# Fused two-block kernel: the last quarter of the first query weights loaded into weight buffer 0, query blocks 12 to 15 at rows 7 to 10

## What is computed

```python
def block(hb):                       # hb: 128 tokens
    q = (hb @ w_pq).reshape(TOK_BLOCK, PEER_HEADS, 2, PEER_DHALF)
    s = jnp.einsum('thpd,hpnd->thpn', q, sub_keys)
    s1, i1 = lax.top_k(s[:, :, 0], PEER_TOPK)
    s2, i2 = lax.top_k(s[:, :, 1], PEER_TOPK)
    ...
    idx = jnp.take_along_axis(cand_i, pos, axis=-1)
    gate = jax.nn.softmax(top_s, axis=-1)
    u = expert_u[idx]
    act = jax.nn.gelu(jnp.einsum('thkd,td->thk', u, hb), approximate=False)
    return jnp.einsum('thk,thkd->td', gate * act, expert_v[idx])
```

## Time and profile before

| | us |
|---|---|
| three timed runs | 2435.77, 2431.96, 2430.18 |
| median | 2431.96 |
| the profiled execution, its own time | 2429.78 |
| its span, first to last instruction | 2428.0 |
| around the span | 1.8 |

### The profile page before, as it was taken

The page is one execution under the profiler, slowest core; times in us unless marked ns, Lnnn a source line. Parts: engine busy times, 40 slices in busy tenths (PEclk is TensorE's granted clock), DMA queues, the critical chain, the costliest instruction groups (busy, mean ns, idle before and its releaser), DMA issues.

```text
span 2428.0 us, 34184 instructions
## 1 busy us (share of the span) xinstructions
PE 2081.3 (86%) x12956; PEld 1589.9 (65%) x12956; DVE 1543.4 (64%) x3428; ACT 1211.8 (50%) x2391; POOL 802.9 (33%) x684
## 2 busy tenths in 40 slices
PE   6989998897797886666669999776998999989998
PEld 4445576786555655555567788645887757858863
DVE  5565665688865677788566686566666544955422
ACT  1123331466657667666676567767776740111110
POOL 2000000365643333455544895333332310800000
PEclk9999888998898998666679999987999999999999
DMA  4322245788899999999999999999999975353431
GB/s 169 121 96 69 73 146 206 285 325 306 352 354 395 415 418 415 420 421 419 417 418 415 414 362 417 415 418 414 409 413 412 412 297 193 113 189 107 172 139 69
DMA packets 162133, 729.71 MB, mean 301 GB/s; under 512 B 10161, under 2 KB 13361, under 8 KB 95921
## 3 DMA queue, kind: packets, MB, share of 16 engines
q0 software_dynamic: 73728, 536.90, 54.7%
q1 hardware_dynamic: 88240, 190.62, 21.5%
HBM read 725.38 MB, written 2.10 MB: 300 GB/s over the span
## 4 chain that ended last, share of the span: by engine, by line
PE 45%; DMA 25%; DVE 15%; ACT 9%; issue 4%; POOL 2%; SPq 0%; DVEq 0%; ACTq 0%; POOLq 0%
DMA AR<-in_uv,C 19%; PE PA L923 12%; PE PD L1510 7%; PE PA L1442 4%; PE PD L923 4%; ACT AR L2026 3%; PE PA L1455 3%; DVE AR L2944 2%; DMA WR<-in_w_up 2%; DMA WR<-in_w_down 2%; DVE AR L2888 2%; PE PD L1087 2%; PE PA L1584 2%; PE PD L1584 2%; POOL AR L3179 1%
## 5 line engine op out<-in xcount | busy, mean ns | idle before, releaser
L2888 DVE CUSTOM_DVE_ANT_0 AR<-AR,HN 128x1024 f32<-128x1024 f32 x467 | 587.9, 1264 | 344.1 <-issue 180.8
L3179 POOL DMA_INDIRECT AR<-in_uv,C x467 | 558.7, 1196 | 711.7 <-PE PD L1510 669.3
L1510 PE MATMUL PD<-C,AR 128*128 128x128 f32 x3736 | 594.0, 313 | 221.1 <-ACT AR L2026 219.9
L1510 PEld LDWEIGHTS PD<-C,AR 128*128 128x128 f32 x3736 | 504.7, 162 | 351.9 <-ACT AR L2026 299.4
L2026 ACT ACTIVATE AR<-AR,SC 128x1024 f32<-128x1024 f32 x467 | 536.6, 1149 | 15.2
L2022 ACT ACTIVATE SC<-SC 128x1 f32<-128x1 f32 x512 | 103.7, 203 | 368.8 <-DVE SC L2888 367.7
L3179 POOL DMA_INDIRECT WR<-in_uv,C x45 | 52.4, 1164 | 464.1 <-DVE C L2621 394.7
L923 PE MATMUL PA<-HT,WR 128*128 128x256 f32 (+1 forms) x608 | 185.2, 465 | 0.9 <-ACT AR L2045 0.9
L1442 PE MATMUL PA<-HT,WR 128*128 128x256 f32 x704 | 168.7, 386 | 12.1 <-DMA WR<-in_w_up 12.1
L923 PE MATMUL PA<-AR,WR 128*128 128x256 f32 (+1 forms) x896 | 170.4, 353 | 0.7 <-ACT AR L1803 0.7
L923 PEld LDWEIGHTS PA<-AR,WR 128*128 128x128 f32 x896 | 152.6, 193 | 17.7 <-ACT AR L1803 1.1
(11 more groups left out here) (495 smaller groups left out, 3088.5 us busy)
## 6 DMA issues: line engine op xcount, KB each, us to landing
WR<-in_w_up SPq DMA_DIRECT2D x22, 2048.0 KB, 18.0
WR<-in_w_in SPq DMA_DIRECT2D x18, 2048.0 KB, 8.5
WR<-in_w_ada SPq DMA_DIRECT2D x12, 2048.0 KB, 8.3
WR<-in_w_down SPq DMA_DIRECT2D x9, 2048.0 KB, 9.4
WR<-in_w_pq SPq DMA_DIRECT2D x8, 2048.0 KB, 16.4
WR<-in_w_o SPq DMA_DIRECT2D x4, 2048.0 KB, 18.4
WR<-in_w_out SPq DMA_DIRECT2D x4, 2048.0 KB, 18.9
AR<-in_uv,C POOLq DMA_INDIRECT x467, 14.6
```

The lines of the kernel that those rows point to most:

```text
L1510: ins = nc.tensor.matmul(acc[i // 4][:, P * (i % 4):P * (i % 4) + P], uv_row(j, D + P * i, D + P * i + P), ident, start=(k == 0 and i % 4 ...
L2888: ttr(uv_row(j, 0, D), uv_row(j, 0, D), HN[:, t, :], 1.0, 0.0, ALU.mult, ALU.add, DOT[:, j:j + 1]).then_inc(s["dots"], 1)
L3179: nc.gpsimd.indirect_dma_start(uv_row(ring_slot(turn), 0, 2 * D), None, uv, bass.IndirectOffsetOnAxis(ap=IDX[:, t % 2, i:i + 1], axis=0),) ...
```

## The change

The fourth quarter of w_pq goes to weight buffer 0 instead of 1, behind the third. So weight buffer 1 is free once block 7 is done, and the ring has places 0, 8, 9, 10, 11 from row 0 to row 51. Blocks 12 to 15 move from rows 2, 2, 3 and 4 to rows 7, 8, 8 and 10, key score 4 from row 7 to row 13, the matrices of chunk 1 from rows 11, 13, 15 to 14, 16, 18 (and so their masks from rows 20, 22, 24 to 23, 25, 27). GpSimd's clear moves from row 5 to row 12 and waits for block 15 in place of block 11. GpSimd's wait for block 15 at row 8 becomes a wait for block 7 at row 3.

```diff
-PHASES = ((0, (8, 9, 0)), (6, (8, 9, 10, 11, 0)), (52, (9, 3, 5, 6, 0, 4, 8)), (66, (7, 3, 5, 6, 0, 4)),
+PHASES = ((0, (0, 8, 9, 10, 11)), (52, (9, 3, 5, 6, 0, 4, 8)), (66, (7, 3, 5, 6, 0, 4)),
           (96, (7, 3, 5, 6, 0, 4, 1, 2)))
...
-MATRIX_AT = {1: (11, 13, 15), 2: (33, 35, 36), 3: (39, 41, 42)}
+MATRIX_AT = {1: (14, 16, 18), 2: (33, 35, 36), 3: (39, 41, 42)}
...
-FIRST_QUERY_AT = {0: (8, 9), 1: (10, 11), 2: (12, 13), 3: (14,), 4: (15,)}
-FIRST_SCORE_AT = {4: 3, 7: 4}
+FIRST_QUERY_AT = {0: (8, 9), 1: (10, 11), 7: (12,), 8: (13, 14), 10: (15,)}
+FIRST_SCORE_AT = {4: 3, 13: 4}
+CLEAR_AT = 12
...
-        col_chunk(w_pq, 512, 512, "a", FIRST_A[("query", 7)])
-        col_chunk(w_pq, 1024, 512, "a", FIRST_A[("f", 3)])
-        col_chunk(w_pq, 1536, 512, "uv", FREED[10] - 1)
-        SLOTS += [1, 2, 0, 3, 1, 0, 1]
+        col_chunk(w_pq, 512, 512, "uv", FREED[10] - 1)
+        col_chunk(w_pq, 1024, 512, "a", FIRST_A[("query", 11)])
+        col_chunk(w_pq, 1536, 512, "a", FIRST_A[("f", 3)])
+        SLOTS += [1, 2, 0, 3, 1, 0, 0]
...
-                if row == 5:
+                if row == CLEAR_AT:
                     own_done()
-                    pool.wait_ge(s["a_full"], FIRST_A[("query", 11)] + 1)
+                    pool.wait_ge(s["a_full"], FIRST_A[("query", 15)] + 1)
                     z = WR[64:128, 0, 0:3072].rearrange("p (i n) -> p i n", i=3 * H)
                     joined(nc.gpsimd.memset(z[:, :, 0:64], 0.0), "cleared")
...
-                    if turn == 8:
-                        pool.wait_ge(s["a_full"], FIRST_A[("query", 15)] + 1)
+                    if turn == 3:
+                        pool.wait_ge(s["a_full"], FIRST_A[("query", 7)] + 1)
```

## The result

| | before | after |
|---|---|---|
| median of 8 runs each, us | 2433.93 (2428.73 to 2438.09) | 2444.51 (2440.82 to 2449.91) |
| ratio, 95% interval | | 1.0046 (1.0032 to 1.0061) |
| the profiled execution, its own time | 2429.78 | 2443.26 |
| its span | 2428.0 | 2441.5 |

The changed kernel is slower by 0.46%, some 10.6 us between the medians (the ratio is not the quotient of the two medians, which would be 1.0043). The two profiled executions differ by 13.5 us. From about L923 on, a line of the code has a number higher by one in the changed kernel (L924, L1088, L1511, L2889, L3137, L3146, L3180 for L923, L1087, L1510, L2888, L3136, L3145, L3179).

A forecast was written before the change was run, and what follows sets the result against it. TensorE's own list was taken to set the pace in rows 0 to 11, VectorE and ScalarE to make it wait after row 16. 9.0 + 2.1 + 2.3 - 4.4 = 9.0 us on 2431 gave 2440, range 2433 to 2448.

The forecast's parts named there:

- More places, gathers early: nothing gained: Dots 4 to 6: removes VectorE's gather waits, which TensorE's blocks cover; gains nothing, at most 10.8 us.
- Blocks out of rows 2 to 4: TensorE idle 1.0 us before row 5: Row 5: TensorE's list ends at 463.5, but the row is ready at 464.5, so TensorE idles 1.0 us.
- Row 8 at 475.9, block 15 done at 490.7: Rows 5 to 10 with the moved blocks: nothing won or lost, as row 11 started at 490.74 before.
- The fourth quarter: no wait: SP's w_pq load before block 12: 19.6 us available, load 16.4 in the middle; no wait taken, at most 11.1 us.
- The clear at row 12: 9.0 us: GpSimd's clear waits for block 15, gather 12 issues at 494.1, row 12 starts at 502.9, 9.0 us late.
- What is still to do and the clock: 2.1 + 2.3 us: Behind row 12: key score 4 and row 11's matrix add 2.1 us, the lower clock after idling 2.3 us.
- What is given back: 4.4 us: Rows 12 to 22: a late TensorE makes its idle time before rows 19 and 22 disappear, 4.4 us, bounds nothing to 6.6.
- Matrices and masks three rows later: no change: Chunk 1's moved masks: each costs a VectorE dot as much at its new row, so the sum stays.
- the delay given back: Rival: rows 13 to 22 make up for more of the gap, 6.6 us; 2435 to 2438 us; chance 0.21.
- the gather waits as pace: Rival: at rows 4 to 6 gather waits set the pace, so 10.8 us come off; 2429 us; chance 0.07.
- the late load: Rival: the fourth quarter's load makes block 12 wait, up to 11.1 us; 2451 us, at 22 us 2442; chance 0.08.
- held gathers: Rival: something else holds gather 3 or 4, and the gap at row 12 stays; still 2440 us; chance 0.02.

The follow-up runs named there:

- Run 4: Changed kernel with the clear at row 17 and the earlier three places in rows 0 to 5: 2440.25 us, 1.0024 of the kernel before.
- run 1: Changed kernel with GpSimd's clear at row 17 in place of row 12: 2431.6 us, 0.9992 of the kernel before.
- run 2: Kernel before with only gather 12 held until TensorE has done row 11's transposes: 2440.83 us, 1.003 of the kernel before.
- run 6: Changed kernel, clear at row 12, with chunk 1's three masks at rows 27, 29 and 31: 2441.16 us, 1.0025 of the kernel before.
- run 5: Changed kernel with the clear at row 17 and chunk 1's three masks at rows 27, 29 and 31: 2426.35 us, 0.997 of the kernel before.
- run 7: Kernel before with only chunk 1's three masks moved to rows 27, 29 and 31: 2433.53 us, 0.9996 of the kernel before.

## Why the prediction was right, and where its working was not

- **More places, gathers early: nothing gained. Right.** The waits ahead of dots 4 to 6 went, and row 5 came when TensorE's list allowed. Run 4 gives the other half: with the blocks moved and the places not, 7.4 us are lost.
- **Blocks out of rows 2 to 4: TensorE idle 1.0 us before row 5. Off by that 1.0.** Row 5 began at 463.27, with no wait in front of it; 464.5 was forecast (0.4 of the difference was there at row 0). The mis-sized term is ScalarE's 3.00 us from table load to end. The table load ran ahead of dot 5, so 1.75 us after the dot (461.13) the scaled line was there, at 462.88, before TensorE had done its list:

```profile
457.78 1.28 ACT L2023 ACT_TABLE_LOAD   x1
...
461.73 1.15 ACT L2027 ACTIVATE AR<-AR,SC 128x1024 f32<-128x1024 f32 x1
```

- **Row 8 at 475.9, block 15 done at 490.7.** 474.73 and 489.54: the durations held, and both are early by the 1.2 us of the point before.
- **The fourth quarter: no wait. Right.** Block 12 followed without idle time, and the eight loads took about what they did before: 8.0 to 29.2 us, 16.8 in the middle.

```profile
472.84 2.05 PE L924 MATMUL PA<-AR,WR 128*128 128x128 f32 x16
```

- **The clear at row 12: 9.0 us. Right.** Gather 12 was issued at 492.86 (forecast 494.1), row 12 began at 502.94 (forecast 502.9). That the two agree so well owes something to chance: the gather left 1.2 us early, and dot 12 took 2.71 us in place of 1.23 because a small mask ran beside it. GpSimd's wait was 21.04 us, a little over the 15 to 20 named as the sign.
- **What is still to do and the clock: 2.1 + 2.3 us. Right in size.** Behind row 12, transposes and right product took 507.93 - 502.94 = 4.99 us against 2.98 at full clock: 2.0 us for the clock, at a granted clock of 0.50 in the stretch 495 to 505 us, which is 1.2 GHz of the two levels, after 8.77 us of idling. The work moved behind row 12 shows in run 1, which comes to row 12 in 50.88 us from row 0 in place of 52.83, 1.95 sooner, and to row 22 within 0.3 us of the time it took before.
- **What is given back: 4.4 us. This step failed; it was nothing.** The idle time ahead of rows 20, 21 and 22 is 0.33 + 2.63 + 2.87 = 5.8 us, where ahead of rows 17, 18, 19 and 22 it had been 0.18 + 0.89 + 1.67 + 2.75 = 5.5 (rows 17 and 18 of the kernel before, then ScalarE's second table load of row 22, before and after):

```profile
509.68 1.09 PE L1510 MATMUL PD<-C,WR 128*128 128x128 f32 x8 [0.18 <-ACT WR L2026]
...
512.73 1.09 PE L1510 MATMUL PD<-C,WR 128*128 128x128 f32 x8 [0.89 <-ACT WR L2026]
```

```profile
524.51 1.28 ACT L2022 ACT_TABLE_LOAD   x1
```

```profile
537.76 1.28 ACT L2023 ACT_TABLE_LOAD   x1
```

I had taken these waits as slack that a late TensorE fills. But they are the lateness of VectorE (dots 19 before and 21 after stand behind masks) and, at row 22, of ScalarE, whose table load ends behind dot 22 in both (525.79 against 524.85, 539.04 against 537.23). Both were held by the same gap: VectorE idled for 16.45 us before dot 12, ScalarE for 15.88 us before the gelu of row 12, and GpSimd's masks stood behind the held clear as well. All start again together and meet as before. Run 1 beside the changed kernel shows it (13.31 us at row 13, 13.30 at row 22), run 2 with nothing else changed (9.22 and 9.23), run 6 beside run 5 with the masks away (13.24 and 13.24, though there only 1.6 us of idle time are left to give). Against the kernel before, the waits of rows 17 to 19 do go in the changed kernel, as their masks come three rows later; row 19 is only 10.05 us behind (527.55 against 517.50). But rows 20 and 21 wait in their stead. The sum without this term, 9.0 + 2.1 + 2.3 = 13.4, is what the traces show (13.25 at row 22).

- **Matrices and masks three rows later: no change. Right**, by the idle time just given. The rule that I took from the Trainium skill ("SBUF — State Buffer", Who interferes with whom), that a two-input VectorE instruction and a GpSimd instruction that reads SBUF exclude one another, agrees with dot 21: 4.01 us beside a mask of 2.36.

The forecast of 2440.0 was so low by the term given back: 2440.0 + 4.4 = 2444.4, against 2444.51. That the two lie so close is chance in part. The forecast counts from 2431, the median before came out at 2433.93, and the medians are 10.6 us apart, not 13.4. The interval of the ratio, 7.8 to 14.8 us, holds 9.0 as well as 13.4; that nothing was given back is known from the traces, not from the time. Of the rivals, the delay given back falls with runs 1, 2 and 6, the gather waits as pace with run 1, the late load with block 12, and held gathers with GpSimd's list, where gathers 3 and 4 leave at 436.54 and 438.63 without waiting for TensorE.

## What to carry to other kernels

A wait on an engine that issues gathers holds every gather behind it, and costs the row that comes when the ring runs dry, plus the clock: put such a wait where its event has already come (run 1: five rows later, 13.3 us). Idle time of one engine is no slack for a delay that holds what it waits for too: here 5.5 us of it took up nothing. And when a ring grows and the work that covered its waits moves, judge the two together: here each undid the other.

## What had not been expected of the hardware

A dot and a mask of GpSimd that overlap don't slow each other down: one goes first, and the other does all its work behind it. GpSimd's masks in the changed kernel beside dots 6, 12, 20, 21 and 22:

```profile
461.95 1.29 POOL L3137 TENSOR_TENSOR AR<-AR 128x512 f32<-128x512 f32 x1
...
498.77 1.27 POOL L3137 TENSOR_TENSOR AR<-AR 128x512 f32<-128x512 f32 x1
...
527.98 1.40 POOL L3137 TENSOR_TENSOR AR<-AR 128x512 f32<-128x512 f32 x1
530.53 2.36 POOL L3146 TENSOR_TENSOR X<-X,C 128x1024 f32<-128x1024 f32 x1
...
534.86 1.28 POOL L3137 TENSOR_TENSOR AR<-AR 128x512 f32<-128x512 f32 x1
```

Beside dots 6, 12, 21 and 22 the masks end at 463.24, 500.04, 532.89 and 536.14, the dots at 464.34, 501.13, 533.98 and 537.23: 1.09 to 1.10 us later each time, nearly a dot's whole length (1.21), though these dots began 0.13 to 0.56 us before the masks. So a dot of 1.21 us beside a mask of 2.36 takes 4.01: its lead is lost too. Dot 20 began 0.95 us before its mask and kept its 1.21 us; there the mask was the longer one, 1.40. Wherever a dot went first, a small mask ended 1.12 to 1.15 us behind it and a long one 2.21 to 2.23. In all nine traces, between 429 and 720 us, a dot that began 0.76 us or more ahead of one of these masks (L3136, L3145) went first; between 0.49 and 0.63 us it went either way; with less the mask did. The profile's starts alone do not settle it, though. In each trace one later product of GpSimd (L3153 in the kernel before, at 664.29 us) began 0.13 to 0.14 us behind a dot (664.16 us) and yet went second: it took 2.22 us where it had taken 1.26 at 632.43, and the dot took 1.23. (Seven dots that stood behind one long mask had GpSimd's next product go first too, at leads of 2.5 to 2.6 us, and took 4.8 to 5.0 us.) This is why moving a mask by some rows can give 4.4 us (run 5). It fits run 7 as well, where dot 8 led its mask by 0.51 us in place of 0.90 and went second.
